# A decoder step on one NeuronCore: low halves of 24 weight pieces by GpSimd, later tanh, and another pace for background work

## The reference, cut to what matters

```
z = rmsnorm(x) @ w_in            # one product; its columns feed four branches and the gates
# B: q, k, v = silu(causal_dwconv(z_gqkv, history, w_gdn))       width 4, 1536 channels ("gx")
# A: o_A = z_ab * causal_dwconv(z_ac * z_ah, history, w_sconv)   width 3, 512 channels ("ah")
# FFN: silu(causal_dwconv(xn @ w_g, history, w_f)) * (xn @ w_u)  width 3, 2816 channels ("fg")
def causal_dwconv(x, hist, w):
    xc = concatenate([hist, x]);  y[t] = sum_j w[j] * xc[t + j]
# C: glu -> causal depthwise conv, width 31                      ("taps")
# D: a sample attends to 2048 past tokens: 8 samples x 16 pages of 128 keys, found by a page table
```

## Time and profile before

| | us |
|---|---|
| median of three runs | 1835.05 (1833.76 to 1837.18) |
| the profiled execution | 1833.14 |
| its span on the core | 1831.3 |

### The profile page before, as it was taken

The page is one execution under the profiler, slowest core; times in us unless marked ns, Lnnn a source line. Parts: engine busy times, 40 slices in busy tenths (PEclk is TensorE's granted clock), DMA queues, the critical chain, the costliest instruction groups (busy, mean ns, idle before and its releaser), DMA issues. The chain is left out here.

```text
span 1831.3 us, 28404 instructions
## 1 busy us (share of the span) xinstructions
PE 1546.3 (84%) x11127; PEld 1424.3 (78%) x11127; DVE 942.1 (51%) x1421; ACT 555.5 (30%) x893; POOL 489.8 (27%) x286
## 2 busy tenths in 40 slices
PE   4896577878797978988899879889577999999996
PEld 4896577678796977877666659888476999999995
DVE  4169877999977754223222222264525566663122
ACT  3322441122224212263222232443214333333222
POOL 1253312234343400001111104310402444443440
PEclk8897786899898989999888879989757999999998
DMA  7145423433453416557343006432312233332331
GB/s 213 47 118 154 127 76 103 125 107 115 116 150 104 133 54 203 147 159 223 115 126 99 24 21 194 127 89 87 127 35 75 81 93 93 93 93 77 98 97 47
DMA packets 250997, 199.86 MB, mean 109 GB/s; under 512 B 11620, under 2 KB 208797, under 8 KB 250456
## 3 DMA queue, kind: packets, MB, share of 16 engines
q1 hardware_dynamic: 234149, 169.47, 31.9%
q10 hardware_dynamic: 15723, 23.86, 3.8%
q0 software_dynamic: 992, 4.72, 0.8%
HBM read 187.89 MB, written 10.81 MB: 108 GB/s over the span
## 5 line engine op out<-in xcount | busy, mean ns | idle before, releaser
L802 PE MATMUL pb<-xh,wh 128*128 128x260 f32 x2176 | 647.8, 298 | 48.7 <-DVE xl L1516 22.6
L802 PE MATMUL pb<-xl,wh 128*128 128x260 f32 x2176 | 631.9, 290 | 0.0
L802 PE MATMUL pb<-xh,rawl 128*128 128x260 f32 x2176 | 630.6, 290 | 0.0
L762 POOL TENSOR_TENSOR rawl<-raw,wh 128x1024 fp32r<-128x1024 f32 (+2 forms) x128 | 277.8, 2171 | 930.5 <-ACT wh L1145 930.3
L802 PEld LDWEIGHTS pb<-xh,wh 128*128 128x128 f32 x2176 | 428.5, 197 | 66.0 <-issue 34.9
L802 PEld LDWEIGHTS pb<-xl,wh 128*128 128x128 f32 x2176 | 428.4, 197 | 0.7
L802 PEld LDWEIGHTS pb<-xh,rawl 128*128 128x128 f32 x2176 | 427.7, 197 | 0.0
L1145 ACT ACTIVATE wh<-raw 128x1024 fp32r<-128x1024 f32 (+2 forms) x208 | 201.6, 969 | 557.0 <-PE pb L802 531.0
L802 PE MATMUL sd<-ar 128*128 128x128 f32 (+5 forms) x1584 | 282.7, 374 | 93.0 <-DVE ar L1516 33.8
L802 PEld LDWEIGHTS sd<-ar 128*128 128x128 f32 (+4 forms) x1584 | 199.9, 199 | 139.6 <-issue 78.1
L773 POOL TENSOR_TENSOR ar<-ar 128x512 f32<-128x512 f32 x128 | 182.2, 1423 | 333.1 <-DMA ar<-in_cache_fox_k 317.3
(11 more groups left out here) (168 smaller groups left out, 1756.9 us busy)
## 6 DMA issues: line engine op xcount, KB each, us to landing
raw<-in_w_in SPq DMA_DIRECT2D x80, 512.0 KB, 4.1
ar<-in_cache_fox_k SPq DMA_DIRECT2D x128, 256.0 KB, 2.7
ar<-in_cache_fox_v SPq DMA_DIRECT2D x128, 256.0 KB, 3.1
raw<-in_w_ffn_in SPq DMA_DIRECT2D x44, 512.0 KB, 3.7
raw<-in_w_branch SPq DMA_DIRECT2D x32, 256.0 KB, 3.2
raw<-in_w_ffn_out SPq DMA_DIRECT2D x16, 512.0 KB, 3.9
ar<-in_cache_mem_k ACTq DMA_DIRECT2D x1, 4096.0 KB, 19.2
raw<-in_w_out SPq DMA_DIRECT2D x8, 512.0 KB, 4.0
```

The lines of the kernel that those rows point to most:

```text
L762: pool.tensor_tensor(rawl[:, p % RING, 0:kt, :], raw[:, p % RING, 0:kt, :], wh[:, p % (AHEAD + 1), 0:kt, :].bitcast(F32), SUB).then_inc(lo ...
L802: return pe.matmul(o, l, r, start=start, stop=stop, skip_group_check=True)
```

## The change

1. `LOW_BY_DVE` loses gx, ac, ah and ab: for pieces 12 to 35, 24 pieces, GpSimd makes the low half.
2. `evac` puts a gx tile's tanh and its last VectorE instruction behind the convolution of the next gx tile. The l2 steps stand one piece later.
3. The first tap of gx and fg tiles is a third copy out of PSUM on ScalarE (with the tap's weight as scale); for ah it stays on VectorE.
4. The samples' past rows times weights are multiplied and summed once, in the prologue (`pasts`), for all three convolutions; `conv` adds one vector of 8 values per tile. In `conv` the third tap waits for the end of the second.
5. The next query is fetched right after the last product of the one before, and the order leaves out one page at each such place.
6. Pace: in pieces 8 to 11, 4 taps per half piece instead of 2; in gx one per piece instead of two; in 24 to 35 three per piece instead of four. K pages: one per half piece before gx and in 24 to 35, one per piece in gx, three per piece from 36 on.

```diff
--- before.py
+++ after.py
@@ -133,7 +133,7 @@
 RING, AHEAD = 5, 2
-LOW_BY_DVE = ("gx", "ac", "ah", "ab", "gateA", "brA", "gateC", "brC", "fk", "fv", "gz", "kv", "cq")
+LOW_BY_DVE = ("gateA", "brA", "gateC", "brC", "fk", "fv", "gz", "kv", "cq")
 PIECE_MT = []
...
@@ -164,7 +164,7 @@
         + [("AFTER", "fq")] + [("fqr", n) for n in range(2)] + [("KSTART",)]
-        + [x for n in range(4) for x in (("AFTER", "gx", 2 * n + 1), ("l2", n))] + [("l2", 4)]
+        + [x for n in range(4) for x in (("AFTER", "gx", min(11, 2 * n + 2)), ("l2", n))] + [("l2", 4)]
         + [("AFTER", "gx")]
...
@@ -215,11 +215,17 @@
     out, pos, step_n, tile, at_piece, bg = [], [0], [0], [0], [-1], {"tap": None, "k": None, "v": None}
+    turned = [False]
     size = {"tap": N_TAP, "k": N_PAGE, "v": len(V_EVENTS)}
...
             if bg[kind] is not None and bg[kind] < size[kind]:
+                if kind == "k" and bg[kind] % PAGES == 0 and bg[kind] > 0 and not turned[0] and n < 10:
+                    turned[0] = True
+                    return
+                if kind == "k":
+                    turned[0] = False
                 out.append(V_EVENTS[bg[kind]] if kind == "v" else (kind, bg[kind]))
...
@@ -253,8 +259,12 @@
         while tile[0] < len(MT_LAST) and MT_LAST[tile[0]] <= upto_piece:
-            out.append(("evac", tile[0]))
-            out.append(("evac2", tile[0]))
+            m = tile[0]
+            out.append(("evac", m))
+            if MT_KIND[m] == "gx" and MT_KIND[m - 1] == "gx":
+                out.append(("evac2", m - 1))
+            if MT_KIND[m] != "gx" or MT_KIND[m + 1] != "gx":
+                out.append(("evac2", m))
             tile[0] += 1
...
@@ -317,8 +327,8 @@
                     out.append(("napply", 2, KD))
-            background("tap", 1 if kind == "gx" else 2)
-            background("k", 1 if kind == "gx" or h == 0 else 1 + p % 2)
+            background("tap", {"cv": 4, "cg": 4, "gx": h, "ac": 2 - h, "ah": 2 - h, "ab": 2 - h}.get(kind, 2))
+            background("k", {"gx": h, "ac": 1, "ah": 1, "ab": 1}.get(kind, 1 if h == 0 or p < first_piece("gx") else 2))
     evac(NP_ - 1)
...
@@ -634,6 +644,10 @@
 
+        gh = cols[:, B_GS:B_GS + 4, 0:72].rearrange("p n (b r) -> p n b r", b=2)
+        sh = cols[:, B_SS, 0:64].rearrange("p (b r) -> p b r", b=NB)
+        fh = cols[:, B_FS:B_FS + 4, 0:88].rearrange("p n (b r) -> p n b r", b=2)
+
         def both(x):
...
@@ -762,15 +776,21 @@
 
+            def query(b):
+
+                pool.dma_start(qb[:, :], qscr[b:b + 1, :].to_broadcast([P, 512])).then_inc(qb_in, 16)
+
             def product(i):
 
+                if i == 0:
+                    pool.wait_ge(qs_out, 16)
+                    query(0)
                 if i % PAGES == 0:
-                    if i == 0:
-                        pool.wait_ge(qs_out, 16)
-                    pool.dma_start(qb[:, :], qscr[i // PAGES:i // PAGES + 1, :].to_broadcast([P, 512])).then_inc(qb_in, 16)
                     pool.wait_ge(qb_in, 16 * (i // PAGES + 1))
...
                 own(pool.tensor_tensor(kring[:, i % 4, :], kring[:, i % 4, :], qb[:, :], MUL), prod_done)
+                if i % PAGES == PAGES - 1 and i < N_PAGE - 1:
+                    query(i // PAGES + 1)
 
...
@@ -1190,6 +1210,9 @@
                                             pb[:, m % 2, 1, TH - n_:TH], ACT.Copy))
+                    y, w = (gx_tile(idx), col(V_GW + 36 + idx)) if kind == "gx" else \
+                        (pairA[:, s, :], cols[:, B_FW, 2 * KF + idx:2 * KF + idx + 1])
+                    act_c.by(act.activation(both(y), x, ACT.Copy, scale=w))
                     fn(both(cb[:, s, 3:3 + T]), x, ACT.Copy, mt_act)
...
@@ -1527,20 +1550,22 @@
 
-            def conv(x, y, width, wcol, hist, w_last, st):
-
-                ts(y, x[:, 3:3 + T], w_last)
+            def conv(x, y, width, wcol, past, st):
+
+                ys = y[:, SEQ:T] if len(past.shape) == 2 else y[:, SEQ:T].rearrange("p (n b) -> p n b", b=2)
                 for j in range(width - 1):
                     if j:
-                        dve.wait_ge(dve_c.sem, dve_c.n - 1)
-                    dve_c.by(dve.scalar_tensor_tensor(out=y[:, 0:SEQ], in0=x[:, 4 - width + j:4 - width + j + SEQ],
-                                                      scalar=wcol(j), in1=y[:, 0:SEQ], op0=MUL, op1=ADD))
-                    past = hist(j)
-                    ys = y[:, SEQ:T] if len(past.shape) == 2 else y[:, SEQ:T].rearrange("p (n b) -> p n b", b=2)
-                    if j:
-                        dve.wait_ge(dve_c.sem, dve_c.n - 1)
+                        dve.wait_ge(dve_c.sem, dve_c.n - (j == 1))
                     (st if j == width - 2 else dve_c).by(dve.scalar_tensor_tensor(
-                        out=ys, in0=past, scalar=wcol(j), in1=ys, op0=MUL, op1=ADD))
+                        out=y[:, 0:SEQ], in0=x[:, 4 - width + j:4 - width + j + SEQ], scalar=wcol(j), in1=y[:, 0:SEQ], op0=MUL, op1=ADD))
+                    if j == 0:
+                        dve_c.by(dve.tensor_tensor(ys, ys, past, ADD))
+
+            def pasts(h, w, width, n):
+
+                tt(h, h, w, MUL)
+                for j in range(1, width - 1):
+                    tt(h[..., 0:n], h[..., 0:n], h[..., j * n:(j + 1) * n], ADD)
 
...
@@ -1570,17 +1595,12 @@
                 elif kind == "gx":
-                    gh = cols[:, B_GS:B_GS + 4, 0:72].rearrange("p n (b r) -> p n b r", b=2)
-
-                    def hist(j):
-                        return gh[:, :, :, j * 12 + idx]
-
-                    conv(cb[:, s, :], gx_tile(idx), GCW, lambda j: col(V_GW + 12 * j + idx), hist, col(V_GW + 36 + idx), ev_y)
+                    conv(cb[:, s, :], gx_tile(idx), GCW, lambda j: col(V_GW + 12 * j + idx), gh[:, :, :, idx], ev_y)
                 elif kind == "ah":
...
                     cp(tail_sc[:, idx, :], cb[:, s, SEQ + 1:SEQ + 11])
-                    conv(cb[:, s, :], pairB[:, s, :], SCW, lambda j: col(V_SW + 4 * j + idx),
-                         lambda j: cols[:, B_SS, 0:64].rearrange("p (b r) -> p b r", b=NB)[:, :, 4 * j + idx], col(V_SW + 8 + idx), ev_all)
+                    ts(pairB[:, s, :], cb[:, s, 3:3 + T], col(V_SW + 8 + idx))
+                    conv(cb[:, s, :], pairB[:, s, :], SCW, lambda j: col(V_SW + 4 * j + idx), sh[:, :, idx], ev_all)
                 elif kind == "ab":
...
@@ -1599,12 +1619,7 @@
                 elif kind == "fg":
-                    fh = cols[:, B_FS:B_FS + 4, 0:88].rearrange("p n (b r) -> p n b r", b=2)
-
-                    def hist(j):
-                        return fh[:, :, :, j * KF + idx]
-                    conv(cb[:, s, :], pairA[:, s, :], FCW, lambda j: cols[:, B_FW, KF * j + idx:KF * j + idx + 1], hist,
-                         cols[:, B_FW, 2 * KF + idx:2 * KF + idx + 1], ev_y)
+                    conv(cb[:, s, :], pairA[:, s, :], FCW, lambda j: cols[:, B_FW, KF * j + idx:KF * j + idx + 1], fh[:, :, :, idx], ev_y)
                 elif kind == "fu":
...
@@ -1936,6 +1951,9 @@
             tt(wsl[:, :, :], wsm[:, :, :], wsh[:, :, :].bitcast(F32), SUB, wsm_lo)
+            for x, w, width, n in ((gh, cols[:, B_VEC, V_GW:V_GW + 36], GCW, 12), (fh, cols[:, B_FW, 0:44], FCW, KF)):
+                pasts(x, w[:, None, None, :].to_broadcast([P, 4, 2, (width - 1) * n]), width, n)
+            pasts(sh, spread(cols[:, B_VEC, V_SW:V_SW + 8], NB, 1), SCW, 4)
             spl = [0]
...
```

## The result

| | kernel before | changed kernel |
|---|---|---|
| median of 8 runs each, same chip | 1834.16 us (1830.67 to 1844.13) | 1846.92 us (1838.66 to 1855.86) |
| ratio | | 1.0063 (95% interval 1.0036 to 1.009) |
| the profiled execution, its span | 1833.14, 1831.3 | 1848.52, 1846.7 |

The change makes the kernel slower by 0.6%, some 12 us. The forecast was 20 us faster, with a range that ends at 1838. It was wrong in sign.

A forecast was written before the change was run, and what follows sets the result against it. VectorE's queue was taken as the bound from 134 to 433 us. Front terms -7-13-21-3 = -44 and later terms +3+21 = +24 gave -20 together, so 1835.05-20 = 1815 us, range 1798 to 1838.

The forecast's parts named there:

- rival 2: GpSimd's subtractions hold VectorE: 57 us of lock against 31 us taken away; 6 us slower, 1841 us, chance 0.11.
- C: The gs pieces (beside the sample state), 272 to 360 us: 66 of 88 us needed, -21 us (ends -15 and -26).
- E: Pieces 36 to 60: taps and pages put off come back on VectorE, +3 us (ends 0 and +12).
- What bounds the kernel: From 134 to 433 us VectorE's queue is the bound, busy 264.1 of 299 us.
- A: First five gx pieces, 134 to 191 us: early taps cost 5.7 us, then tiles regain 12.7; -7 us (ends -2 and -14).
- B: Next seven gx pieces, 191 to 272 us: 4.3 us for each of three l2 steps, -13 us (ends -8 and -23).
- D: First DeltaNet chunk, 360 to 433 us: TensorE's holes are mostly the chain's, -3 us (ends 0 and -10).
- F: Forced flush at piece 61: K pages 113 to 127 are still unmultiplied, +21 us (ends +10 and +43).
- Rivals 1 and 3: Flush mostly hidden or front gains at their ends: 1804 us, chance 0.17; every front part at its low end: 1834, 0.12.
- Rival 4: GpSimd, behind page waits, delivers low halves late and TensorE waits; gains of 20 us to 272 us gone, 1835 us, chance 0.05.

## Why the prediction was wrong, by its own steps

The step that failed is the weighing of GpSimd's subtractions: their lock stood in rival 2 alone and at nothing in the sum, since VectorE "can stand still" for it. It costs 22 us there. Of the 32.5 us between the forecast and the measured place of piece 62 (-20 and +12.5), 20.5 go when VectorE makes the low halves; the 12 that stay are nearly all in C and E.

**What bounds the kernel**: right in the main. With the low halves left to VectorE the measured front is -40.1 where -44 was forecast. But it is VectorE's place in the chain as much as its load: the later tanh alone, which takes no work off it, gives -23.3 at piece 36.

**A, -7, measured +4.4.** The failed term is the taps and what they hold. The 15 taps were priced at 0.87 us and their lateness at one arrival, 5.7 us. But a tap took 1.24 us in the mean (1.15 for the 33 ahead of the first gx convolution), that convolution begins 10.2 us later than before (168.26 and 158.05), and each reduction behind four of them frees the slot behind which SyncE holds the weights. Taking away the early taps or the subtractions, each by itself, brings -6.8 and -6.7.

**B, -13, measured -16.3.** Right, and the later tanh alone does it (-14.8 between pieces 17 and 24). It was put down to the l2 chain, as in the earlier trace rows.

**C, -21, measured -8.0.** The working took "7x1.31 less" for VectorE and no lock. Without the subtractions it is -14.3, so 6.7 us of the miss are not the lock's: the gs pieces then take 73.7 us where 67 were added up, two terms of them by estimate. The sums over the state begin at 281.6, not at 259; 8 of these 23 us are the lateness of piece 24, from A.

**D, -3, measured -1.0**; -4.3 without the subtractions. Right in size.

**E, +3, measured +11.** The count was nearly right (8 taps, 7 pages by the emitted order), the price wrong. I read "VectorE idles 20.5 of 127 us" as room. With the subtractions, both old paces lose 0.6 between pieces 36 and 61, the old page pace alone 4.8 (so the 8 taps cost 4.3), the old pace of taps alone 9.2 (so the pages cost 8.6). My reading, not tested by itself: the idle time of a chain is spread over waits for other engines, and work put there lengthens the chain. The +12 end of the range held it.

**F, +21, measured +22.4.** Right, and by the mechanism told: 5.5 us a round of four was forecast (1.38 a page), 1.43 a page measured (and 16 pages in piece 61, one more than I counted). Of the 1.43, 1.26 are GpSimd's product, so the ring's round and GpSimd's own pace can't be told apart. That only GpSimd and the next page set the pace, and TensorE had no cover, was right too.

**The rivals.** Rival 2 was the one, at a chance of 0.11, with its sign, its mechanism and its place, and the range stopped 9 us short of the result. Its price was 26 us on the path (57 of lock less 31 of relief), giving 1841. Measured, taking the 24 subtractions back is worth 0.0121 of 1834, 22 us, near that; what is missing to 1847 is mostly E. That the size agrees is partly luck, for the price hangs on what stands around: by the ratios the same 24 subtractions cost 2 us in the kernel before, 14 with the later tanh, 10 with both old paces and the new convolution, 6 with the new taps besides, and 22 in the changed kernel. What was wrong is the argument against it: "VectorE then has only some 5 us of work per piece, so it can stand still". In the changed kernel it was busy 57 of 61 us over the first five pieces, since the locked time is busy time, and taps had just been put there. And the lock needs no full engine to cost: at the l2 steps it lengthens links of a chain that TensorE waits for at its end. In the kernel before, where the l2 steps stood for the tanh anyway and VectorE was full besides, lock and relief seem to cancel (1.0013, while twelve idle subtractions cost 0.0043); the relief is concluded from these two. Rivals 1 and 3 had no part: the flush was not hidden, the front not at its low end for want of l2 gain. Rival 4 had none in the changed kernel either, but what it says is real: in the four runs in which GpSimd subtracts at the old page pace, TensorE waits 9.7 to 12.4 us for low halves. It was the slower page pace, with a page left out at each new query, that kept them in time: at the new page pace no run has such a wait for GpSimd.

**The accounting of pages and taps.** The forecast valued pages put off at their VectorE time in the front (0.68) and at less behind. Measured: with VectorE's low halves 20 pages between pieces 12 and 36 are worth 14.8 us, 0.74 each; 14 pages between 48 and 61 cost 0.74 each; the 16 of the flush 1.4 each. Put off, a page gains nothing; flushed, it costs double. This is the second fault.

What stays open: why the two faults together cost 12 us more than their sum. By the places it is 9.5 us at piece 61, and it comes late: 8.6 at piece 17, where early taps, late reductions, locked taps and late weights may feed one another, but -3.5 at piece 24, and 5.9 at piece 36. What the places do show is where the subtractions cost:

| cost of the subtractions by GpSimd, us | pieces 12 to 17 | 17 to 24 | 24 to 36 |
|---|---|---|---|
| new paces | 10.3 | -1.6 | 9.6 |
| new pace of taps, old of pages | 4.1 | -0.2 | 10.9 |
| old paces | 0.8 | 10.5 | 0.2 |

With the old paces the price falls in the l2 steps, with the new pace of taps ahead of them and behind. That the pace of taps moves it is shown; by what wait, from 24 to 36, is not.

## What to carry to other kernels

Price work that moves to GpSimd twice: the time it takes off VectorE, and its own duration as a stand-still of the VectorE operations with two SBUF inputs (and some others, as the copy here) beside it. In none of five surroundings did it pay here, though VectorE was full in some, and an idle instruction of the same shape measures the second price by itself. Before background work is put off, find the stretch where it costs less than where it stands; an engine's idle share in a stretch of chained steps is no such proof. First change the order (here a tanh that blocked ScalarE's queue: 17 us for a few lines), since it moves no work at all.

## What the runs showed of the hardware that was not expected

- The lock works both ways and whole instructions at a time: a tap of 0.74 us takes 1.75 beside a product and 2.84 to 2.93 beside a subtraction, a GpSimd product of 1.29 takes 1.69 in the mean among them, while reductions stay at 0.675. A copy of 38 columns goes from 0.27 to 1.16. Even an addition over 8 columns of 0.16 us takes 1.24 (198.45 in the run with both old paces).
- Twelve GpSimd subtractions of 2.3 us that nobody reads cost the program 8 us in one kernel and 17 in another.
